# Places of the branch operands in a Strassen-style gate stage of a diffusion block: loads, sums and merges re-placed

## What is computed

```python
y_b = u * sv.reshape(B, N, B_WIDTH)
merged = (jax.nn.sigmoid(ga_raw) * jnp.einsum('bne,ed->bnd', y_a, w_pa)
          + jax.nn.sigmoid(gb_raw) * jnp.einsum('bne,ed->bnd', y_b, w_pb))
return jnp.einsum('bnd,de->bne', merged, w_out)
```

## Time and profile before

| what | value |
|---|---|
| median of 3 runs (lowest, highest) | 1801.54 us (1800.96, 1802.07) |
| the profiled execution | 1801.4 us, its span 1799.7 us |
| mean granted TensorE clock | 0.99 |
| PE busy | 1739.4 us (97% of the span) |
| DVE busy | 1157.3 us (64%) |
| ACT busy | 651.1 us (36%) |
| POOL busy | 186.3 us (10%) |
| DMA | 219.29 MB, mean 122 GB/s |
| the stage of 16 blocks | 692.35 to 1028.54 us of the span |

### The profile page before, as it was taken

One profiled execution on the slowest core, in us unless ns is written; L12 is line 12 of the kernel. 1 busy time (PEld: TensorE's weight loads), 2 busy tenths in 40 slices (PEclk: granted clock), 3 DMA queues, 4 the chain that ended last, 5 costly groups with the idle time before them and its releaser, 6 DMA issues.

```text
span 1799.7 us, 23320 instructions
## 1 busy us (share of the span) xinstructions
PE 1739.4 (97%) x8523; PEld 1461.1 (81%) x8523; DVE 1157.3 (64%) x1755; ACT 651.1 (36%) x1033; POOL 186.3 (10%) x244
## 2 busy tenths in 40 slices
PE   6899999999999997999898999999999999999997
PEld 3698988989898886878786888888888888888886
DVE  4677636465557756675778846865656656566667
ACT  6534231423224232445544413443433333221112
POOL 1002020201022000011122200000000001222210
PEclk9999999999999998999999999999999999999999
DMA  7211111102077113884866633132222222722212
GB/s 307 70 49 35 60 47 55 62 23 71 24 252 274 48 71 114 287 304 137 279 200 212 196 130 129 47 113 75 71 93 70 89 97 70 274 112 93 93 47 94
DMA packets 112616, 219.29 MB, mean 122 GB/s; under 512 B 7026, under 2 KB 75778, under 8 KB 108194
## 3 DMA queue, kind: packets, MB, share of 16 engines
q1 hardware_dynamic: 95874, 161.57, 26.4%
q0 software_dynamic: 16672, 56.77, 9.1%
HBM read 168.98 MB, written 49.33 MB: 121 GB/s over the span
## 4 chain that ended last, share of the span: by engine, by line
PE 83%; DVE 7%; DMA 6%; ACT 2%; issue 2%; SPq 0%; DVEq 0%; ACTq 0%; POOLq 0%
PE PD L2244 14%; PE PD L2671 11%; PE PM L2671 11%; PE PD L2691 7%; PE PM L2691 6%; PE PM L2545 5%; PE PD L2545 4%; PE PD L2576 4%; PE PD L2354 4%; PE PD L2260 4%; PE PM L2427 2%; DMA y_ring<-yb_dram 2%; DMA y_ring<-yT_dram 2%; DMA y_ring<-ya_dram 1%; PE PM L2606 1%
## 5 line engine op out<-in xcount | busy, mean ns | idle before, releaser
L2244 PE MATMUL PD<-R_hi,whi 128*128 128x512 f32 x352 | 110.1, 394 | 0.0
L953 POOL TENSOR_TENSOR w_raw<-w_raw,g2B 128x2048 f32<-128x2048 f32 x11 | 50.8, 4622 | 558.8 <-DMA w_raw<-in_w_ff 394.8
L2244 PE MATMUL PD<-R_lo,whi 128*128 128x512 f32 x352 | 108.7, 390 | 0.0
L2244 PE MATMUL PD<-R_hi,wlo 128*128 128x512 f32 x352 | 108.5, 389 | 0.0
L2030 DVE TENSOR_TENSOR ws_lo<-S,ws_hi 128x512 fp32r<-128x512 f32 x76 | 56.3, 742 | 77.2 <-ACT ws_hi L1357 77.2
L2244 PEld LDWEIGHTS PD<-R_hi,wlo 128*128 128x128 f32 x352 | 66.1, 188 | 14.0
L2244 PEld LDWEIGHTS PD<-R_lo,whi 128*128 128x128 f32 x352 | 66.1, 188 | 14.0
L2244 PEld LDWEIGHTS PD<-R_hi,whi 128*128 128x128 f32 x352 | 65.2, 188 | 13.0 <-issue 0.2
L2260 PE MATMUL PD<-whi,R_hi 128*128 128x256 f32 x256 | 72.8, 284 | 0.8 <-ACT vaug L1046 0.8
L2260 PE MATMUL PD<-wlo,R_hi 128*128 128x256 f32 x256 | 72.4, 283 | 0.0
L2260 PE MATMUL PD<-whi,R_lo 128*128 128x256 f32 x256 | 72.4, 283 | 0.0
(11 more groups left out here) (492 smaller groups left out, 5014.0 us busy)
## 6 DMA issues: line engine op xcount, KB each, us to landing
rawF<-in_w_ff SPq DMA_DIRECT2D x44, 512.0 KB, 4.9
ada<-in_w_ada POOLq DMA_DIRECT2D x32, 512.0 KB, 5.6
raw<-in_w_in SPq DMA_DIRECT2D x30, 512.0 KB, 4.6
g_dram<-snapG POOLq DMA_DIRECT2D x48, 256.0 KB, 3.4
f_dram<-Fo SPq DMA_DIRECT2D x11, 1024.0 KB, 4.7
w_raw<-in_w_ff SPq DMA_DIRECT2D x11, 1024.0 KB, 5.0
f_raw<-f_dram SPq DMA_DIRECT2D x11, 1024.0 KB, 6.9
ada_raw<-in_w_ada SPq DMA_DIRECT2D x8, 1024.0 KB, 19.3
```

The source lines that it names most:

```text
L953: nc.gpsimd.tensor_tensor(w2_raw[par], w2_raw[par], g2B[:, :].unsqueeze(1).to_broadcast([P, 2, D]), ALU.mult)\
L2244: i = mm(dst[:, e * HALF:e * HALF + width], wk[:, k, :], part, start=(k == 0 and step == 0), stop=(k == KT - 1 and step == 2))
```

## The change

Three edits. **(1)** `y_ring` holds two whole places, and only places 3 and 6 pass through it. Places 0, 1, 2, 4 and 5 are loaded, 1 MB at a time, straight into the place of their own low part, once product n of block 7 (11) is done; the low part is then made in place. SP then waits for product (8, 1) ((12, 1)) before it goes on to the weights of block 10 (14). High and low parts are made 128x2048 at a time, in the order 0, 3, 1, 2, 4, 5, 6, from product 2 of the fill block on. **(2)** The eight units of sums stand five products apart, from (0, 5) to (5, 5). **(3)** Merges no longer follow their combine: those of blocks 8, 11, 12, 13 and 14 are made in the block after (`MERGE_AT`), those of blocks 9, 10 and 15 stay in their own, the first of 9 and 15 later than their combine. `m_move`, `m_hi` and `m_lo` follow.

The diff, without the lines that only rename arguments:

```diff
+FILL_ORDER = (0, 3, 1, 2, 4, 5, 6)
+UNIT_AT = ((0, 5), (1, 3), (2, 1), (2, 6), (3, 4), (4, 2), (5, 0), (5, 5))
+MERGE_AT = {(9, 0): (0, 1), (9, 2): (2, 3), (9, 3): (4,), (9, 4): (5,), (9, 5): (6,), (9, 6): (7,),
+            (10, 1): (8,), (10, 4): (9,), (10, 5): (10,), (10, 6): (11,), (12, 4): (12, 13), (12, 5): (14, 15),
+            (13, 0): (16, 17), (13, 2): (18, 19), (14, 0): (20, 21), (14, 2): (22, 23),
+            (15, 0): (24, 25), (15, 2): (26, 27), (15, 3): (28,), (15, 4): (29,), (15, 5): (30,), (15, 6): (31,)}
...
-            return y_ring[:, j % 4 // 2, j % 2 * 2:j % 2 * 2 + 2, :]
+        IN_RING = (3, 6)
+        def place_f32(n):
+            return y_ring[:, IN_RING.index(n), :, :] if n in IN_RING else gate_right_lo[n].bitcast(F32)
...
-            def place_load(j):
-                fill, n, at = j // (2 * PRODUCTS), j // 2 % PRODUCTS, slice(j % 2 * 2, j % 2 * 2 + 2)
-                if j < 2:
-                    sp.wait_ge(branch_ready, UNITS)
-                elif j < 4:
+            def place_load(fill, n):
+                if n in IN_RING:
                     sp.wait_ge(sums_out, 16 + 16 * UNITS)
+                    if fill:
+                        sp.wait_ge(branch_ready, UNITS + FILL_ORDER.index(n) + 1)
                 else:
-                    sp.wait_ge(branch_ready, UNITS + j - 3)
+                    sp.wait_ge(product, FILL[fill] * PRODUCTS + n + 1)
...
-                sp.dma_start(ring_slot(j), src[:, at, :]).then_inc(place_in[j % 4], 16)
+                sp.dma_start(place_f32(n), src).then_inc(place_in[n], 16)
...
-                if b < UNITS // 2:
-                    sums_turn(2 * b)
-                    sums_turn(2 * b + 1)
-                if b == UNITS // 2:
-                    for j in range(4):
-                        place_load(j)
+                for u in range(UNITS):
+                    if UNIT_AT[u][0] == b:
+                        sums_turn(u)
+                if b == FILL[0] - 1:
+                    for n in IN_RING:
+                        place_load(0, n)
                 if b in FILL:
-                    for j in range(4, 12):
-                        place_load(FILL.index(b) * 2 * PRODUCTS + j)
-                if b - 1 in FILL:
-                    for j in range(12, 18 if b - 1 == FILL[0] else 14):
-                        place_load(FILL.index(b - 1) * 2 * PRODUCTS + j)
+                    for n in range(PRODUCTS):
+                        if n not in IN_RING:
+                            place_load(FILL.index(b), n)
+                    sp.wait_ge(product, (b + 1) * PRODUCTS + 2)
+                if b == FILL[0] + 2:
+                    for n in IN_RING:
+                        place_load(1, n)
...
-            def branch_hi(fill, part):
-                j, at = fill * 2 * PRODUCTS + part, slice(part % 2 * 2, part % 2 * 2 + 2)
-                act.wait_ge(place_in[j % 4], 16 * (j // 4 + 2))
-                act.wait_ge(product, FILL[fill] * PRODUCTS + part // 2 + 1)
-                nc.scalar.activation(gate_right_hi[part // 2][:, at, :], ring_slot(j), ACT.Copy).then_inc(branch_hi_d, 1)
+            def branch_hi(fill, n):
+                act.wait_ge(place_in[n], 16 * (fill + 2))
+                act.wait_ge(product, FILL[fill] * PRODUCTS + n + 1)
+                nc.scalar.activation(gate_right_hi[n], place_f32(n), ACT.Copy).then_inc(branch_hi_d, 1)
...
-            HI_AFTER = {0: (0, 1), 1: (2, 3), 3: (4, 5), 4: (6,), 5: (7,), 6: (8,)}
-            HI_LATER = {0: (9,), 1: (10, 11), 2: (12,), 3: (13,)}
-            M_HI_AFTER = {0: (0, 1), 1: (2, 3), 3: (4,), 5: (5, 6)}
+            HI_AFTER = {2: 0, 3: 3, 4: 1, 5: 2}
+            HI_LATER = {0: 4, 1: 5, 2: 6}
+            M_HI_AFTER = {0: (0, 1), 1: (2,), 3: (3, 4), 5: (5, 6)}
...
-                    if b in (GB - 3, GB - 2) and n < 4:
-                        m_move(b - 1, n)
+                    if b in (GB - 3, GB - 2) and n >= 3:
+                        m_move(b - 1, n - 3)
...
-            LO_AFTER = {1: (0, 1), 2: (2, 3), 4: (4, 5), 5: (6,), 6: (7,)}
-            LO_LATER = {0: (8, 9), 1: (10,), 2: (11, 12), 3: (13,)}
-            M_LO_AFTER = {1: (0, 1), 2: (2, 3), 3: (4,), 6: (5, 6)}
+            LO_AFTER = {3: 0, 4: 3, 5: 1, 6: 2}
+            LO_LATER = {1: 4, 2: 5, 3: 6}
+            M_LO_AFTER = {1: (0, 1), 2: (2,), 3: (3,), 4: (4,), 6: (5, 6)}
...
-                        if b >= GATES:
-                            merge(b, SUM_AFTER[n])
...
-                    if b < UNITS // 2 and n in (1, 5):
-                        branch_sums(2 * b + n // 5)
+                    if (b, n) in UNIT_AT:
+                        branch_sums(UNIT_AT.index((b, n)))
...
+                    for q in MERGE_AT.get((b, n), ()):
+                        merge(GATES + q // 4, q % 4)
...
-                        pe.wait_ge(branch_ready, UNITS + fill * 2 * PRODUCTS + 2 * n + 2)
+                        pe.wait_ge(branch_ready, UNITS + fill * PRODUCTS + FILL_ORDER.index(n) + 1)
```

More of the change, by code:

```diff
@@ L369, in m_part @@
             return snapG[4 * (at // 2 - 2) + SNAP_OF[quad_of(at % 2, e)]][:, :].unsqueeze(1)
-        def ring_slot(j):
-            return y_ring[:, j % 4 // 2, j % 2 * 2:j % 2 * 2 + 2, :]
+        IN_RING = (3, 6)
+        def place_f32(n):
+            return y_ring[:, IN_RING.index(n), :, :] if n in IN_RING else gate_right_lo[n].bitcast(F32)
         def m_place(R, n):
@@ L550, in build @@
         out_done = sem("out_done")
-        sums_in, sums_out, place_in = ada_in[0], ada_in[1], ada_in[2:6]
+        sums_in, sums_out, place_in = x_in[LT], x_in[LT + 1], ada_in[0:PRODUCTS]
         block = es.enter_context(nc.Block())
@@ L1252, in m_move @@
                 if cb + i == 0:
-                    act.wait_ge(branch_ready, UNITS + 4 * PRODUCTS)
+                    act.wait_ge(branch_ready, UNITS + 2 * PRODUCTS)
                 nc.scalar.activation(y_ring[:, cb, 2 * m + e, :], snapG[4 * cb + SNAP_OF[i]][:, :], ACT.Copy)\
@@ L1294, in _ @@
                         gate_tanh(b, n // 3 - 1)
-                    if b in FILL:
-                        for part in HI_AFTER.get(n, ()):
-                            branch_hi(FILL.index(b), part)
-                    if b - 1 in FILL:
-                        for part in HI_LATER.get(n, ()):
-                            branch_hi(FILL.index(b - 1), part)
-                    if b in (GB - 3, GB - 2) and n < 4:
-                        m_move(b - 1, n)
+                    if b in FILL and n in HI_AFTER:
+                        branch_hi(FILL.index(b), HI_AFTER[n])
+                    if b - 1 in FILL and n in HI_LATER:
+                        branch_hi(FILL.index(b - 1), HI_LATER[n])
+                    if b in (GB - 3, GB - 2) and n >= 3:
+                        m_move(b - 1, n - 3)
                     if last:
@@ L1907, in branch_sums, with branch_lo @@
                 v.tensor_tensor(t4, b21, t2, ALU.subtract).then_inc(branch_ready, 1)
-            def branch_lo(fill, part):
-                j, n, at = fill * 2 * PRODUCTS + part, part // 2, slice(part % 2 * 2, part % 2 * 2 + 2)
-                dve.wait_ge(branch_hi_d, j + 1)
-                v.tensor_tensor(gate_right_lo[n][:, at, :], ring_slot(j), gate_right_hi[n][:, at, :].bitcast(F32),
-                                ALU.subtract).then_inc(branch_ready, 1)
+            def branch_lo(fill, n):
+                dve.wait_ge(branch_hi_d, fill * PRODUCTS + FILL_ORDER.index(n) + 1)
+                v.tensor_tensor(gate_right_lo[n], place_f32(n), gate_right_hi[n].bitcast(F32), ALU.subtract)\
+                    .then_inc(branch_ready, 1)
             def merge(b, i):
@@ L1963, in _ @@
                             gate_left_sums(b + 1, [s[:, :, :] for s in gS], True)
-                    if b < UNITS // 2 and n in (1, 5):
-                        branch_sums(2 * b + n // 5)
-                    if b in FILL:
-                        for part in LO_AFTER.get(n, ()):
-                            branch_lo(FILL.index(b), part)
-                    if b - 1 in FILL:
-                        for part in LO_LATER.get(n, ()):
-                            branch_lo(FILL.index(b - 1), part)
+                    if (b, n) in UNIT_AT:
+                        branch_sums(UNIT_AT.index((b, n)))
+                    if b in FILL and n in LO_AFTER:
+                        branch_lo(FILL.index(b), LO_AFTER[n])
+                    if b - 1 in FILL and n in LO_LATER:
+                        branch_lo(FILL.index(b - 1), LO_LATER[n])
+                    for q in MERGE_AT.get((b, n), ()):
+                        merge(GATES + q // 4, q % 4)
                     if last:
```

## The result

| | kernel before | changed kernel |
|---|---|---|
| median (lowest, highest) of 7 runs each, us | 1802.07 (1800.96, 1804.52) | 1808.45 (1806.48, 1811.15) |
| ratio to before, 95% interval | | 1.0034 (1.0023 to 1.0046) |
| profiled execution, span, us | 1801.4, 1799.7 | 1811.15, 1809.5 |
| stage of 16 blocks, first matmul to output projection | 692.35 to 1028.54 | 694.53 to 1037.67 |

What follows compares the result with a forecast made beforehand. PE was taken as the bound (97% busy). Sums -2.6, fills -4.7, block 13 +2.0 and end +1.7 made -3.6 against the profiled 1801.4, so 1797.8 us; range 1792.5 to 1805.

Steps and rivals of the forecast that it cites:

- Sums, -2.6: Block 4: with sums spread five products apart, the whole 2.57 us lost there goes; bounds 0 to -2.6.
- A fill loses D - 5.3: Blocks 7-8 and 11-12: loss per fill, D being time from T, the first block's start, to place 0's landing; 5.7 us.
- I take D = 11.0 for both fills: Blocks 7 and 11: place 0 lands 11.0 us after the block's start: weights 7.6, its 1 MB 2.6, gate's store 0.7.
- -4.7: Both fills together: 11.4 us lost instead of 16.1; bounds -7.9 to +2.7.
- the term of 2.6 us for the 1 MB behind them: Blocks 7 and 11: place 0's 1 MB lands 2.6 us after the weights ahead of it on SP.
- The bound of D = 14.7: Fills: latest landing of place 0, from a 10.5 us landing in the trace; a fill would then lose 18.8 for two.
- the slower rival: Fills: place 0 lands at T+15 or more, PE stands still at (7, 5), 9.7 us lost per fill, 1805.8 us; chance 0.14.
- Block 13, +2.0: First snapshot of block 13 waits for block 11's merges and store, counted from F, the start of (12, 6): 2.0 us lost.
- The upper bound of 4.6: Block 13: most it would lose, 4.6 us, if a store takes 6.0 us.
- End, +1.7: End of block 15 and output projection: deferred merges make the output's low parts late, 1.0 and 0.7 us; bounds +0.4 and +3.
- somewhat late: Rival for the fills: place 0 lands at D about 13, 7.7 us lost per fill, 1801.8 us; chance 0.18.
- the gap at (7, 5): Sign on PE in block 7: a gap there would mean place 0 landed after T+11.2.

Runs made afterwards that it cites:

- run 4: The kernel before with only the sums spread over blocks 0 to 5: 1798.66 us, ratio 0.9982.
- run 1: The changed kernel with the weights of blocks 9 and 13 issued behind the loads of places 0, 1 and 2: 1801.27 us, ratio 0.9996.
- run 2: The changed kernel with SP issuing place 1's load only once place 0 has landed: 1807.91 us, ratio 1.0037.
- runs 3 and 9: The changed kernel with every merge behind its combine, 1802.15 us; and the same with weights of blocks 9 and 13 loaded after places 0 to 2, 1796.96 us.

## Why the prediction was wrong

- **Sums, -2.6: right.** -2.57 in the changed kernel, 19.03 for block 4 in run 4.
- **"A fill loses D - 5.3": right.** By D the changed kernel's fills should lose 7.4 and 10.2; they lose 7.60 and 10.22. The same holds without merges in the fill wherever D was changed: 4.1 against 4.17 and 6.3 against 6.36 (run 1), 7.2 against 7.35 and 10.4 against 10.47 (run 2). With merges at once add 0.8 in the first fill and 3.7 in the second (runs 3 and 9 alike).
- **"I take D = 11.0 for both fills": wrong, the first failed step.** It measured 12.7 and 15.5, which costs 1.9 and 4.5 us: -4.7 became +1.75. In the first fill the weights landed at T+7.6 as the sum has it; what failed is the term of 2.6 us for the 1 MB behind them (3.3 with the gate's store), which measured 5.1. It came from four half loads that were all under way when the last landed. Place 0 landed 9.8 us after issue behind 1 MB of weights and 5.7 without them, so the weights cost it 4.1. The bound of D = 14.7 and the slower rival came from the right row, a 10.5 us landing when weights, ring and merge traffic met.
- **One D for two fills: wrong.** In the second fill the weights landed at T+11.4 and not at T+7.6: they were issued 2.0 us later after T and took 7.3 us instead of 5.6. I had costed what the deferral does behind the fills and not ahead of them. With a ring of two quads a merge that is late asks for its next quad late; DVE waits 13 times for 19.4 us, and SP behind it. That is 1.9 us of D2 (15.46 against 13.60). The argument against the slower rival, that the merges are deferred, did not hold: block 8's merges now stand in block 9, those of blocks 9 and 10 still in their own, and place 0 took 10.8 us from its issue with the deferral and 10.4 without.
- **Block 13, +2.0: the mechanism was right, the size was not; the second failed step.** The chain merge, store, snapshot, (13, 3) came as written. With F at 969.61, the merges were to be done by F+7.8 and were at F+9.7; the store was to land at F+11.8 and landed at F+14.2. These 2.4 us are, to 0.1, three parts: 0.9 on POOL, which issued the loads of gates 14 and 15 at F+3.3 and F+4.4 instead of F+2.4 and F+3.5; 0.8 in the load of gate 15, 4.5 us instead of the median of 3.7 in the earlier trace rows; and 0.8 in the store, 4.2 instead of 3.4, with the weights of block 15 issued 0.9 us behind it. A gap of 3.9 instead of 2.0 then took the clock down as well, 2.9 us more, which the step did not have at all. The upper bound of 4.6 was too low for the same reasons.
- **End, +1.7: right**, 1.32 and 0.6 for 1.0 and 0.7.
- **Of the rivals** the one that ends slower described the second fill: D of 15.5 where it asks for 14.7, ACT stuck ahead of a snapshot, PE standing still at (11, 5) for 4.2 us. The first fill was the "somewhat late" one, with the gap at (7, 5), 855.54, that was to show a landing after T+11.2. Neither had block 13 at 6.8. Slower by more than 0.2% had a chance of 0.14, too little for a sum with two terms that rested on landing times at a busy moment.

By terms, in the profiled executions: 6.4 us of the miss are the fills (-4.7 forecast, +1.75 measured), 4.8 block 13, 0.2 the end.

## What to carry to other kernels

When a load is the first link of a chain, look what stands ahead of it on its queue, and price it by landings from moments as busy as the one it will have; where buffers loaded ahead are few, they belong to the operands that are wanted first. Work that is deferred keeps its place in every chain that feeds it: with a ring of two, deferring one merge delays the load of the next, and the engine waits elsewhere. Two edits can cost more together than the sum of their parts (here 9.8 us, where alone one cost nothing and the other 3.5), so an edit of several parts is best timed as a square.
